# Early output projection in the last group sweep, and the group norm's factors applied to y where it is split

## The reference, cut to what matters

```python
# y: (tokens, 2048), from the scans in both directions, 8 groups of 4 heads
y = y + xs * d_skip
y = y * silu(z)
y = y.reshape(b, n, 8, 256)
y = y * lax.rsqrt(jnp.mean(y * y, axis=-1, keepdims=True) + RMS_EPS)   # a factor per group and token
y = y.reshape(b, n, 2048) * norm_g
out = y @ w_out                                                        # (2048, 1024)
x = x + gate * rms(out, post_g)
```

## Time and profile before

| | us |
|---|---|
| median of 3 runs | 2245.79 (2245.78 to 2250.84) |
| profiled execution | 2252.08 |
| its span | 2250.3 |
| sweeps 0 to 6 and the backward half of the last one | 164.7 to 1128.4 |
| forward half of the last sweep, to the next stage | 1128.4 to 1198.5 |
| output stage, first pass (tiles 0 and 1) | 1198.5 to about 1258 |

### The profile page before, as it was taken

The page is one execution under the profiler, slowest core; times in us unless marked ns, Lnnn a source line. Parts: engine busy times, 40 slices in busy tenths (PEclk is TensorE's granted clock), DMA queues, the critical chain, the costliest instruction groups (busy, mean ns, idle before and its releaser), DMA issues. The chain is left out here.

```text
span 2250.3 us, 35627 instructions
## 1 busy us (share of the span) xinstructions
PE 2078.7 (92%) x12426; PEld 1711.4 (76%) x12426; DVE 1401.3 (62%) x3286; ACT 1117.9 (50%) x2742; POOL 467.5 (21%) x451
## 2 busy tenths in 40 slices
PE   5799999999999999999976999898999999999797
PEld 2588888787878878787754888687878878878576
DVE  4475968879596887959585533424555555555652
ACT  4344738566573856647373322324444444444431
POOL 1012323233232323323220111211110110110300
PEclk9899999999999999999987999999999999999799
DMA  9522322222221222222126433132221221221533
GB/s 355 225 66 70 105 67 94 74 76 66 77 92 56 95 75 76 66 77 97 38 80 230 131 121 113 63 79 60 74 59 59 81 59 53 81 57 44 156 82 86
DMA packets 122012, 208.89 MB, mean 93 GB/s; under 512 B 30300, under 2 KB 80476, under 8 KB 119788
## 3 DMA queue, kind: packets, MB, share of 16 engines
q1 hardware_dynamic: 110316, 164.67, 23.4%
q10 hardware_dynamic: 11520, 41.95, 5.5%
HBM read 175.69 MB, written 28.65 MB: 91 GB/s over the span
## 5 line engine op out<-in xcount | busy, mean ns | idle before, releaser
L419 PE MATMUL sg_pP<-h_h_hi,h_whi 128*128 128x512 f32 (+1 forms) x1152 | 429.0, 372 | 4.7 <-PEq L68 4.7
L421 PE MATMUL sg_pP<-h_h_hi,h_wlo 128*128 128x512 f32 (+1 forms) x1152 | 410.1, 356 | 0.0
L420 PE MATMUL sg_pP<-h_h_lo,h_whi 128*128 128x512 f32 (+1 forms) x1152 | 409.4, 355 | 0.0
L419 PE MATMUL h_pP<-h_h_hi,h_whi 128*128 128x512 f32 (+1 forms) x640 | 254.5, 398 | 5.5 <-ACT at_vv L2118 5.3
L419 PEld LDWEIGHTS sg_pP<-h_h_hi,h_whi 128*128 128x128 f32 x1152 | 219.2, 190 | 34.3 <-issue 5.2
L421 PEld LDWEIGHTS sg_pP<-h_h_hi,h_wlo 128*128 128x128 f32 x1152 | 219.0, 190 | 31.5
L420 PEld LDWEIGHTS sg_pP<-h_h_lo,h_whi 128*128 128x128 f32 x1152 | 219.5, 191 | 29.6
L421 PE MATMUL h_pP<-h_h_hi,h_wlo 128*128 128x512 f32 (+1 forms) x640 | 239.2, 374 | 0.0
L420 PE MATMUL h_pP<-h_h_lo,h_whi 128*128 128x512 f32 (+1 forms) x640 | 237.7, 371 | 0.0
L866 ACT ACTIVATE sg_S<-sg_rowb,sg_tab 128x128 f32<-128x128 f32 x640 | 195.9, 389 | 61.0 <-DVE sg_E L1130 54.4
L2232 POOL TENSOR_TENSOR h_wlo<-h_wr,h_whi 128x1024 fp32r<-128x1024 f32 x31 | 74.0, 2387 | 539.5 <-ACT h_whi L2103 539.5
(11 more groups left out here) (358 smaller groups left out, 4517.7 us busy)
## 6 DMA issues: line engine op xcount, KB each, us to landing
sg_rowb<-crows ACTq DMA_DIRECT2D x80, 512.0 KB, 3.7
h_wr<-in_w_ssd SPq DMA_DIRECT2D x48, 512.0 KB, 3.3
fs_w<-in_ada_w SPq DMA_DIRECT2D x16, 1024.0 KB, 8.8
h_wr<-in_w_na SPq DMA_DIRECT2D x32, 512.0 KB, 3.4
at_bias<-bt SPq DMA_DIRECT2D x256, 64.0 KB, 2.3
md_yr<-y SPq DMA_DIRECT2D x40, 256.0 KB, 3.2
fs_w<-in_ada_w SPq DMA_DIRECT2D x16, 512.0 KB, 7.5
y<-sg_Z SPq DMA_DIRECT2D x16, 512.0 KB, 3.2
```

What stands on the lines that cost most here:

```text
L419: pe.matmul(out, w_hi[:, k, :], h_hi[:, k, t0:t0 + n], start=(k == 0), stop=False)
L420: pe.matmul(out, w_hi[:, k, :], h_lo[:, k, t0:t0 + n], start=False, stop=False)
L421: x = pe.matmul(out, w_lo[:, k, :], h_hi[:, k, t0:t0 + n], start=False, stop=(k == KT - 1))
```

## The change

It has two parts. **Factors.** The chunk's norm no longer multiplies Z. GpSimd adds the two halves of the squares (`halves`), TensorE sums them by one product into column c of a row of ten (`norms`), and once a sweep VectorE makes ten variances (`variances`) and GpSimd ten factors (`factor`), which go to a small DRAM tensor `yf` (`store_factors`). Z is stored as gated. Whoever splits y loads the factors of its part, broadcast over the partitions, and multiplies the raw part by them on GpSimd first.

**Early projection.** In the forward half of the last sweep the first nine of the 16 steps of the output projection of tiles 0 and 1 are done (`out_products`, one step in each chunk from c = 1 on), and the weights of the tenth are split (`OUT_DONE, OUT_READY = 9, 10`). y's parts for it are split in slots 10, 10, 11, 12, 15 and 16. `middle` goes on from step 9. All PSUM banks are now allocated once (`banks`), so that the sums stay.

In GpSimd's loop `halves` stands behind `inputs_forth(g, c + 1)` and ahead of `split_lo`. The core of the diff, first `ssd_groups`:

```diff
-        def norm_bank(c): return pA[0]
+        def sums(g):
+            return pA[0][:, (g % 2) * NCH:(g % 2 + 1) * NCH]
+        ow_raw = [past[:, i * D:(i + 1) * D] for i in range(RO)]        # RO = 4, past: the free half of X
+        oparts = [(t, q) for q in range(3) for t in range(2)]
+        part_slot = [FIRST, FIRST, FIRST + 1, FIRST + 2, FIRST + 5, FIRST + 6]      # FIRST = 10
+        obank = [pP, [pA[1], pT]]
 # SyncE
             def store(g):
-                    sp.wait_ge(fin, NCH * g + hi)
+                    sp.wait_ge(fin1, NCH * g + hi)
+            def store_factors(g):
+                sp.wait_ge(rs, g + 1)
+                if g:
+                    sp.wait_ge(rso, 16 * g)
+                sp.dma_start(rs_dram[g].rearrange("(c p) -> p c", p=P), rstd[:, g, :], allow_slow_non_contiguous=True).then_inc(rso, 16)
                     store(g - 1)
+                    store_factors(g - 1)
+            sp.dma_start(ng[:, :], scale).then_inc(ong, 16)
+            for k in range(OUT_READY):
+                if k >= RO:
+                    sp.wait_ge(owls, k - RO + 1)
+                sp.dma_start(ow_raw[k % RO], w_out[k * P:(k + 1) * P, :]).then_inc(owl[k % RO], 16)
+                for i in {0: (0, 1), 1: (2,), 2: (3,), 6: (4, 5)}.get(k, ()):
+                    t, q = oparts[i]
+                    if i >= 2:
+                        sp.wait_ge(oyls, i - 1)
+                    sp.dma_start(oy_raw[i % 2], y_dram[:, q * HY:(q + 1) * HY, t * P:(t + 1) * P]).then_inc(oyl[i % 2], 16)
+                    sp.dma_start(rsb[:, i % 2, :, :], rs_dram[2 * q:2 * q + 2, t * P:(t + 1) * P].partition_broadcast(P)
+                                 ).then_inc(oyl[i % 2], 16)
+            sp.wait_ge(oysc, len(oparts))
+            sp.dma_start(wr[...], w_out[OUT_READY * P:(OUT_READY + 1) * P, :]).then_inc(owx, 16)
             store(G - 1)
...
             for b in range(NBL):
                 sp.wait_ge(yst[b], 16 * G)
+            store_factors(G - 1)
 # TensorE
+            def out_products(k):
...
+                pe.wait_ge(owls, k + 1)
+                for t in range(2):
+                    i = oparts.index((t, k // HY))
+                    if k % HY == 0:
+                        pe.wait_ge(oyls, i + 1)
+                    for lo, wlo_ in ((0, 0), (0, 1), (1, 0)):
+                        for h in range(2):
+                            x = pe.matmul(obank[t][h][:, :], oy[lo][i][:, k % HY, :],
+                                          ow[wlo_][:, k, h * (D // 2):(h + 1) * (D // 2)], ...)
+                x.then_inc(odone, 1)
             def norms(g, c):
-                if 0 <= c - 2 < NCH:
-                    pe.wait_ge(dg, n - 1)
-                    if n >= 3:
-                        pe.wait_ge(fin, n - 2)
-                    pe.matmul(bank[:, P:2 * P], ones[:, :], diag[:, :], start=True, stop=True).then_inc(bcs, 1)
-                if 0 <= c - 1 < NCH:
-                    pe.wait_ge(sqs, n)
-                    if n >= 2:
-                        pe.wait_ge(vr, n - 1)
-                    for t in range(PAIRS):
-                        x = pe.matmul(bank[:, 0:1], sq[:, t * P:(t + 1) * P], ones[:, 0:1], ...)
-                    x.then_inc(ssm, 1)
+                n = g * NCH + c - 2
+                if c >= 2:
+                    pe.wait_ge(sqa, n + 1)
+                    if c == 2 and g >= 2:
+                        pe.wait_ge(vr, g - 1)
+                    pe.matmul(sums(g)[:, c - 2:c - 1], sqh[:, :], ones[:, 0:1], start=True, stop=True).then_inc(ssm, 1)
                     forth_state(g, c)
                     if units[g][NCH + c] is not None:
                         unit(units[g][NCH + c])
+                    if g == G - 1 and c >= 1:
+                        out_products(c - 1)
 # ScalarE
             def square(g, c):
-                    act.wait_ge(ssm, n)
+                    act.wait_ge(sqa, n)
+            def out_parts(s):                    # at the end of each slot of the last forward half
+                k = s - FIRST
+                if k == 0:
+                    act.wait_ge(ong, 16)
+                    act.wait_ge(pj, NBL * len(tiles))
+                for i in range(len(oparts)):
+                    if part_slot[i] == s:
+                        act.wait_ge(oysc, i + 1)
+                        if i >= 4:
+                            act.wait_ge(odone, HY)
+                        act.activation(oy[0][i], oy_raw[i % 2], ACT.Copy).then_inc(oyh, 1)
+                act.wait_ge(owl[k % RO], 16 * (k // RO + 1))
+                act.activation(ow[0][:, k, :], ow_raw[k % RO], ACT.Copy, scale=ng[:, k:k + 1]).then_inc(owh, 1)
 # GpSimd
-            def factor(g, c):
-                pool.wait_ge(vr, g * NCH + c + 1)
...
-                pool.tensor_tensor(rstd[:, :], var[:, :], mhalf[:, :], ALU.pow).then_inc(rs, 1)
+            def halves(g, c):
+                n = g * NCH + c
+                pool.wait_ge(sqs, n + 1)
+                if n:
+                    pool.wait_ge(ssm, n)
+                pool.tensor_tensor(sqh[:, :], sq[:, 0:P], sq[:, P:UN], ALU.add).then_inc(sqa, 1)
+            def factor(g):
+                pool.wait_ge(vr, g + 1)
+                pool.tensor_tensor(rstd[:, g, :], var[:, :], mhalf[:, 0:1].to_broadcast([P, NCH]), ALU.pow).then_inc(rs, 1)
+                    if c >= 1:
+                        halves(g, c - 1)
+                    if g and s == 0:
+                        halves(g - 1, NCH - 1)
+                    if g and s == 2:
+                        factor(g - 1)
+                    for i in range(len(oparts)):
+                        if g == G - 1 and part_slot[i] == s:
+                            pool.wait_ge(oyl[i % 2], 32 * (i // 2 + 1))
+                            yg = oy_raw[i % 2].rearrange("p (g k) c -> p g k c", g=2)
+                            pool.tensor_tensor(yg, yg, rsb[:, i % 2, :, :]..., ALU.mult).then_inc(oysc, 1)
+                            pool.wait_ge(oyh, i + 1)
+                            pool.tensor_tensor(oy[1][i], oy_raw[i % 2], oy[0][i].bitcast(F32),
+                                               ALU.subtract).then_inc(oyls, 1)
 # VectorE: norm_early and norm_late (L1185, L1190, L1200) go
+            def variances(g):                    # in slot 2 of the next sweep
+                dve.wait_ge(ssm, (g + 1) * NCH)
+                if g:
+                    dve.wait_ge(rs, g)
+                dve.tensor_scalar(var[:, :], sums(g), 1.0 / UN, EPS, ALU.mult, ALU.add).then_inc(vr, 1)
+                    if g == G - 1 and c >= 0:    # at the end of each slot
+                        if c == 0:
+                            dve.wait_ge(ong, 16)
+                        dve.wait_ge(owh, c + 1)
+                        dve.scalar_tensor_tensor(ow[1][:, c, :], ow_raw[c % RO], ng[:, c:c + 1], ow[0][:, c, :].bitcast(F32),
+                                                 ALU.mult, ALU.subtract).then_inc(owls, 1)
```

and `middle`, in which the loads of the gates now stand behind step 12's weights (they stood behind step 4's) and that of x behind step 14's (8's):

```diff
-        y_with = {0: (0, 1), 1: (2,), 2: (3,), 3: (4,), 4: (5,), 7: (6, 7), 11: (8, 9), 15: (10, 11)}
+        y_with = {10: (6, 7), 12: (8,), 13: (9,), 15: (10, 11)}
+        Y0, YF0 = 6, 4
+        K0 = OUT_READY
             def load_y(i):
...
+                if q == 3:
+                    sp.wait_ge(rso, 16 * GROUPS)
+                sp.dma_start(factors_of(i), rs_dram[2 * q:2 * q + 2, t * P:(t + 1) * P].partition_broadcast(P)
+                             ).then_inc(yl[i % 2], 16)
-            for k in range(kt):
-                load_w(k)
+            for k in range(K0, kt):
+                if k > K0:
+                    load_w(k)
...
-            for k in range(kt):
-                pe.wait_ge(wls, k + 1)
+            for k in range(OUT_DONE, kt):
+                if k >= K0:
+                    pe.wait_ge(wls, k - K0 + 1)
                 for t in range(2):
                     products(t, k)
             def y_hi(i):                         # ScalarE
-                act.wait_ge(yl[i % 2], 16 * (i // 2 + 1))
+                act.wait_ge(ysc, i + 1 - Y0)
 # GpSimd, for every part from 6 on; those of tile t + 2 behind the two powers of tile t
+            def scaled(i):
+                pool.wait_ge(yl[i % 2], 32 * ((i - Y0) // 2 + 1))
+                yg = yr[:, i % 2, :, :].rearrange("p (g k) c -> p g k c", g=2)
+                pool.tensor_tensor(yg, yg, factors_of(i)..., ALU.mult).then_inc(ysc, 1)
```

205 lines of the change are left out of this document (110 added, 95 removed).

## The result

The changed kernel takes 2248.97 us in the median of 20 runs (2244.83 to 2254.32), the kernel before 2245.78 (20 runs, 2241.21 to 2250.84): a ratio of 1.0017, interval 1.0010 to 1.0025. Forecast were 2196 us, range 2175 to 2224. So nothing was gained where 50 us were expected (the change is 0.17% slower), and the time lies outside the range. The profiled execution took 2251.29 us, its span 2249.5.

What follows compares the result with a forecast made beforehand. TensorE was taken to bound sweeps 0 to 6, VectorE's chain the last forward half, w_out's loading and splitting and TensorE the output head; -38 + 22 - 4.5 - 30 = -50.5 us from 2245.8 gave 2196 us, range 2175 to 2224.

Steps and rivals of the forecast that it cites:

- What bounds the kernel: TensorE in sweeps 0 to 6, a VectorE chain in the last forward half, w_out loading, splitting and TensorE at output head.
- Part 1: Norms of sweeps 0 to 6: fewer TensorE products and shorter waits give -38 us, from -25 to -48.
- I cost it at 0: GpSimd's 0.45 us addition per chunk in the sweeps: work queued behind it has 6 us or more, so no cost.
- to about 95: VectorE's busy time in a sweep falls from 101 of 129 us to about 95, 0.6 us less a chunk.
- Part 2: Last forward half: nine early projection steps lengthen VectorE's chain and slots that split y, +22 us, from +18 to +32.
- one behind the other: Slot 10 of the last forward half: two parts of y in series, 4.6 us extra.
- Part 3: End of the last sweep: the store can start at the last L1176, -4.5 us.
- Part 4: Head of the output stage: only steps 9 to 15 of 16 are left, -30 us, from -25 to -33.
- I take 3 us, from 1.6 to 8: Output stage head: the time for the last factors' store of 1280 single elements, a form in no row.
- Later: Rest of the output stage: old order, GpSimd's 34 multiplications lie beside long steps, 0 us, to +3.
- B: Rival: GpSimd and VectorE hold each other up, +15 us in the last forward half, 2211 us; chance 0.15.
- D: Rival: GpSimd's addition holds the next chunk's inputs for TensorE, +208 us over 80 chunks, 2403 us; chance 0.03.

Runs made afterwards that it cites:

- e4: The changed kernel with TensorE summing both halves of the squares itself and GpSimd's addition gone: 2216.8 us, ratio to before 0.9862.
- e9: The changed kernel with TensorE's one product summing a constant tile, and GpSimd's addition and its waits gone: 2206.7 us, ratio to before 0.9818.
- e10: e9 with GpSimd's addition and its waits put back, TensorE not waiting for it: 2253.0 us, ratio to before 1.0018.
- e5: e4 with GpSimd keeping its wait for the end of TensorE's chunk, adding nothing: 2231.5 us, ratio to before 0.9940.
- e3: The changed kernel with GpSimd multiplying only two of 128 columns of y's parts in the last forward half: 2243.3 us, ratio to before 0.9984.
- e2: The changed kernel with factors stored as ten rows of 512 bytes, not 1280 single elements: 2241.1 us, ratio to before 0.9979.
- e14: The changed kernel without early projection, two sums on TensorE, factors stored as rows, first-pass multiplications cut to two columns: 2216.2 us, ratio to before 0.9856.
- e13: e10 without the addition itself, GpSimd keeping only its two waits: 2232.1 us, ratio to before 0.9926.

## Why the prediction failed, point by point

*What bounds the kernel:* right for TensorE in the sweeps (from e4 to e9, with one product a chunk less and no wait for the squares, they fall by 11.4 us) and for VectorE's chain in the slots of the last half without a part of y; those with one went by the chain between GpSimd and ScalarE, as the prediction says further on. The sweep of 129 us on which it goes was a window that is not a whole sweep; a sweep took 131.

*Part 1, norms of the sweeps, -38 us.* The step that failed is "I cost it at 0" for GpSimd's addition: with its waits it cost 28.2 us (e9 to e10). e9, in which the addition and its waits don't exist, gives -41.3 in place of -38; after gives -13.4. That 41.3 is near 38 doesn't prove the terms: in e9 TensorE waits for no squares, its waits for the sum of outputs still grew from before's 6.9 us to 15.2, and the 2.86 us convolutions of before are gone, which the sum didn't know of. I had asked only who waits for the addition (nobody in the sweeps, which e10 confirms to 0.3 us) and not what runs beside it. That VectorE would fall by 6 us a sweep, "to about 95", failed for the same reason: it lost 29 instructions a sweep and 1.1 us.

*Part 2, last forward half, +22.* It was +33.1, above its range too. (By its own terms, 19 and a third of five slow steps of 2.7 us, the sum is 23.6 and not 22.) The mechanism was the one foreseen, the sizes were not: slots without a part of y take 7.1 us (forecast 6.55) and those with one 10.3, 12.6, 11.3 and 12.3 (forecast 9.1), slot 10 15.6 (forecast 11.2). The engines in slot 10 of after, from the first multiplication on:

```profile
1108.41 1.34 POOL L1123 TENSOR_TENSOR sg_X<-sg_X,h_wr 128x512 f32<-128x512 f32 x1
1116.53 0.61 ACT L977 ACTIVATE h_whi<-sg_X 128x512 fp32r<-128x512 f32 x1
1117.22 1.66 POOL L1126 TENSOR_TENSOR h_wlo<-sg_X,h_whi 128x512 fp32r<-128x512 f32 x1 [7.46 <-ACT h_whi L977]
1117.67 1.75 DVE L1181 SCALAR_TENSOR_TENSOR sg_Z<-sg_th,sg_Z 128x512 f32<-128x512 f32 x1
1118.84 1.70 POOL L1123 TENSOR_TENSOR sg_X<-sg_X,h_wr 128x512 f32<-128x512 f32 x1
...
1122.35 1.28 DVE L1369 SCALAR_TENSOR_TENSOR h_h_lo<-sg_X,sg_ng,h_h_hi 128x1024 fp32r<-128x1024 f32 x1 [2.92 <-ACT h_h_hi L979]
...
1123.73 1.19 PE L783 MATMUL h_bank<-h_h_hi,h_whi 128*128 128x512 f32 x2 [8.08 <-DVE h_h_lo L1369]
```

The terms were taken at their undisturbed durations: the second multiplication takes 1.70 us, not 1.29, and L1181 beside GpSimd 1.75, not 0.69. The first multiplication was ready 6.8 us before ScalarE, which splits y only at the end of its slot, came to it; then the second part waited for the low half of the first, which is what the prediction had as "one behind the other". The wait for TensorE's chunk, which I had in the sum, is the largest piece that a run took out: 10.6 us (e4 to e5, two products). The multiplications are 6.8 (e3).

*Part 3, end of the sweep, -4.5.* From the last gating to the next block 6.1 us, before 9.26: -3.1. The power of ten columns, which I took at 1 us, takes 2.0 there.

*Part 4, head of the output stage, -30.* From its first issue to the squares 43.8 us in place of 59.1: -15.3. The step that failed is the store of single elements, "I take 3 us, from 1.6 to 8": the load behind it went 10.7 us later, beyond my upper bound, and the norm's gains, which don't need it, were late as well; e2's rows give 8.7 us back. With rows some 6 us of the difference to the forecast stay open. GpSimd's multiplications may be part of them: three of the six take 2.3 us and not 1.29. e14 shows for the kernel without the early projection that these cost time, 4.4 us; with it they weren't taken out.

*Later, 0 to +3:* +2.7, but kernels with the same later stages spread over 989 to 996 us, so this is no finding.

*The rivals.* B, that GpSimd and VectorE hold each other up, named the right mechanism for the sweeps, and I mispriced it: 15 us in the last half alone and nothing in the sweeps, where 28 us lay with the waits (e9 to e10). In the last half the wait counts for most (10.6 us to e5, 8.2 from e9 to e13) and the addition for less (1.2 us with two products, 5.5 with one). What I held against B, that the removed power of one column was GpSimd work too, was no argument: no run shows whether that power held VectorE up. And B's price could have been read from the trace of before, where 13 convolutions took 2.86 us in place of 0.75 beside L968; I looked only at GpSimd's L985. The Trainium skill, "SBUF — State Buffer", section "Who interferes with whom", says that a VectorE instruction with two SBUF inputs contends with a GpSimd instruction that reads SBUF, and one with at most one SBUF input, outside VectorE's two-port modes, does not. By that rule the trace agrees: the convolutions, two inputs in SBUF, went from 0.484 to 0.77 us beside GpSimd, and L1250, one input in a matmul's bank, kept 0.68, in the 23 cases beside GpSimd as in the 57 others. D, that GpSimd's addition holds TensorE's inputs back, did not come: the wait for sg_xdb went from 11.3 to 13.5 us only.

*Range and chances.* 0.94 for faster rested on sums in which every new operation of GpSimd had its undisturbed duration. The store's upper bound should have come in with its tail, since no row had its form.

## What to carry to other kernels

Before work is moved to an engine that looks idle, read what that engine will run beside, not only who waits for it: here an addition for whose result no engine was late in the sweeps cost 28 us with its waits, and giving TensorE its second product back, in place of that addition, made the kernel 30 us faster than before, where the change had made it no faster. An instruction that takes 2.86 us here and 0.75 there, in a trace that one already has, is the price of such a meeting. A change of two parts should be tried in its parts, with each of them on a base without the shared cost: the early projection looks like a loss of 5 us in after and is a gain of 12 to 13 us without the addition and its waits. And a small store of single elements ahead of a chain of loads made both loads late here, the one that needs it and one that doesn't; turned to rows it cost 2.6 us in place of 10.7.

## What the runs showed of the hardware

- A VectorE instruction with two inputs in SBUF took 1.75 us in place of 0.69 beside a GpSimd instruction of 1.66 us, and GpSimd's took 1.70 in place of 1.34 in the same slot (after).
- Before, a VectorE convolution that started 0.09 us behind a GpSimd instruction of 2.39 us took 2.86 us in place of 0.75 and ended 0.56 us behind it. VectorE's instructions with one input in a matmul's bank kept 0.68 us beside GpSimd (L1250, 23 cases).
- 5 KB stored as 1280 single elements let the next dependent load go 10.7 us later, as ten rows of 512 bytes 2.6 us later; an independent load of 8 KB issued behind the store was waited for until 9.2 us after its issue, in place of 1.7.
- GpSimd's power of 128x10 takes 1.96 to 2.16 us, some four times that of one column (0.55).
- Waits alone, with no work added, cost 14.1 us over seven sweeps (e9 to e13): they move GpSimd's other instructions in time, and VectorE's same 1385 instructions took 9.7 us more.
